# Opening of an expert layer: the residual turned once, the router on the residual, shift and scale applied where gathered rows are turned back

## The reference, cut to what matters

```python
xl = xl + ml[2] * yl                                    # yl = o @ gdn_w_o
hl = _modulate(_rmsnorm(xl, norm_g[1, 1]), ml[3], ml[4])  # h * (1 + scale) + shift
xl = xl + ml[5] * moe(hl)

def moe(h):
    top_v, top_i = lax.top_k(h @ router, 2)
    top_w = softmax(top_v)
    return sum(gate[:, e] * swiglu(h, w_in[e], w_out[e]) for e in range(8))
```

## Time and profile before

| what | value |
|---|---|
| time before, median of 3 | 2807.66 us (2806.9 to 2814.33) |
| the profiled execution, its own time | 2807.92 us |
| its span, first to last instruction | 2805.8 us |
| busy: PE, PEld, DVE, ACT, POOL | 2677.2, 1790.9, 1001.7, 664.5, 523.0 us |
| mean granted TensorE clock | 0.976 |

### The profile page before, as it was taken

How to read it: one execution, slowest core, us unless ns; L and a number is a source line. 1 busy time by engine, 2 the same in 40 slices (tenths; PEclk the granted TensorE clock), 3 DMA queues, 4 the chain that set the end, 5 groups by cost and what they waited for, 6 DMA issues and landing times. The chain is left out here.

```text
span 2805.8 us, 46230 instructions
## 1 busy us (share of the span) xinstructions
PE 2677.2 (95%) x18826; PEld 1790.9 (64%) x18827; DVE 1001.7 (36%) x2298; ACT 664.5 (24%) x1395; POOL 523.0 (19%) x465
## 2 busy tenths in 40 slices
PE   6999999889999999999999999999998999999997
PEld 3555555555555555556677767776557778677784
DVE  2344454227667763113444434443331110000100
ACT  3344444121222210114231333233131010010000
POOL 0111111023233214313233313232100000000000
PEclk8999999899999999999999999999988999999999
DMA  7224222213433332201001110111139995684821
GB/s 241 66 74 124 66 66 77 90 45 90 120 105 110 114 108 70 62 23 32 24 9 32 32 31 2 32 32 31 39 118 368 307 311 185 193 262 156 271 94 31
DMA packets 315616, 297.56 MB, mean 106 GB/s; under 512 B 5824, under 2 KB 277312, under 8 KB 315328
## 3 DMA queue, kind: packets, MB, share of 16 engines
q1 hardware_dynamic: 309408, 273.17, 31.9%
q0 software_dynamic: 4896, 17.83, 2.4%
q10 hardware_dynamic: 1152, 4.19, 0.4%
HBM read 281.01 MB, written 12.58 MB: 105 GB/s over the span
## 5 line engine op out<-in xcount | busy, mean ns | idle before, releaser
L1751 PE MATMUL bank<-work,weight_ring 128*128 128x128 f32 (+1 forms) x2048 | 314.8, 316 | 6.1 <-ACT work L1802 6.1
L2202 PE MATMUL bank<-hidden,weight_ring 128*128 128x512 f32 (+1 forms) x768 | 308.7, 536 | 1.8 <-ACT work L2546 1.8
L1751 PEld LDWEIGHTS bank<-work,weight_ring 128*128 128x128 f32 x2048 | 291.2, 193 | 27.7 <-issue 8.1
L640 PE MATMUL bank<-weight_ring,hidden 128*128 128x384 f32 x760 | 267.6, 497 | 4.8 <-ACT work L768 4.6
L1292 PE MATMUL bank<-hidden,weight_ring 128*128 128x384 f32 x704 | 238.3, 492 | 4.9 <-ACT hidden L425 4.9
L1438 DVE SCALAR_TENSOR_TENSOR weight_ring<-weight_ring,silu_c 128x256 f32<-128x256 f32 x308 | 213.7, 734 | 5.5
L640 PEld LDWEIGHTS bank<-weight_ring,hidden 128*128 128x128 f32 x760 | 138.3, 191 | 109.2 <-ACT work L768 16.6
L1292 PEld LDWEIGHTS bank<-hidden,weight_ring 128*128 128x128 f32 x704 | 133.2, 192 | 93.7 <-issue 7.0
L2202 PEld LDWEIGHTS bank<-hidden,weight_ring 128*128 128x128 f32 x768 | 134.9, 190 | 82.4 <-issue 68.1
L1292 PE MATMUL bank<-weight_ring 128*128 128x384 f32 x528 | 182.3, 496 | 0.3 <-DVE work L1446 0.3
L1908 DVE TENSOR_TENSOR work<-work,bank 128x128 f32<-128x128 f32 (+1 forms) x88 | 29.7, 338 | 424.6 <-ACT work L1807 424.6
(11 more groups left out here) (364 smaller groups left out, 3774.6 us busy)
## 6 DMA issues: line engine op xcount, KB each, us to landing
weight_ring<-in_moe_w_in SPq DMA_DIRECT2D x64, 1024.0 KB, 9.6
weight_ring<-in_ada_w SPq DMA_DIRECT2D x38, 1024.0 KB, 5.3
weight_ring<-in_ffn_w_in SPq DMA_DIRECT2D x44, 512.0 KB, 4.9
hidden<-in_moe_w_out SPq DMA_DIRECT2D x8, 2816.0 KB, 9.9
residual<-in_moe_w_out SPq DMA_DIRECT2D x8, 2816.0 KB, 15.3
work<-in_moe_w_in SPq DMA_DIRECT2D x16, 1024.0 KB, 8.2
weight_ring<-in_na_w_qkv SPq DMA_DIRECT2D x24, 512.0 KB, 7.8
weight_ring<-in_gdn_w_qkv SPq DMA_DIRECT2D x24, 512.0 KB, 5.5
```

The costliest lines, as they stand in the source:

```text
L640: mm = nc.tensor.matmul(m.psum[6][:, 0:3 * P], m.H[:, k, t * P:(t + 1) * P], weights(u)[:, k, :], start=(k == 0), stop=(k == KD - 1))
L1751: mm = nc.tensor.matmul(B[c % 4][:, ab * HALF:ab * HALF + N], w[:, ab, k, (c % 2) * P:(c % 2 + 1) * P], XG[:, k, 0:N], start=(k == 0), sto ...
L2202: mm = nc.tensor.matmul(B[b][:, c0:c0 + t1 - t0], W[:, s, k, :], m.H[:, k, t0:t1], start=(k == 0), stop=(k == KD - 1))
```

## The change

`finish_output` and the last `Norm` go; their work moves into one Block of `experts` in another order.

- The last products and sums (8 each) stand first in `experts`. `X` is turned once, into eight banks (`X_BANKS`), four blocks of features 0 to 3 for each token tile, then 4 to 7; VectorE alone copies the banks into `RT`.
- ScalarE squares the 4 row tiles of 1024 with an accumulated sum, takes the root, VectorE the reciprocal (`ss`, a value for each row).
- `HT` (now in the `hidden` tensor) is `RT` times `ss`: ScalarE tiles 1 and 3, VectorE 0 and 2. Scale and shift are not in it.
- The router runs on the unnormalised `X`, with the scale multiplied into its weights by GpSimd, as four column groups of 32; shift times router is a matmul of its own (`C_ONES`); the logits get `ss` and the shift part on VectorE.
- Scale and shift are applied in `turn`, as 8 ScalarE instructions with a scale and a bias operand in place of 4 copies; TensorE's first chunk waits for them pair by pair.
- SP: slabs 1 to 3 at once, slabs 0 and 4 once the last products are done, slab 5 after the first gather and the store of `out`, then `w_out`.
- ScalarE stores the four tiles of hidden rows after the exponential of the weights, then copies the gains, then stores the four tiles of `out`.

```diff
@@ sync
-            for j in range(SLOTS):
+            for j in range(1, SLOTS):
                 load_slab(0, j)
-            sp.wait_ge(h_stored, 64)
+            sp.wait_ge(last_product, last_0 + KD)
+            load_slab(0, 0)
             load_slab(0, 4)
+            for b in range(2):
+                sp.wait_ge(gathered[b], 16)
             sp.wait_ge(rows_stored, 64)
             load_slab(0, 5)
-            sp.wait_ge(h_turned, 8)
-            sp.wait_ge(logits, 1)
+            sp.wait_ge(h_stored, 64)
             load_out(0, 0)
@@ gpsimd
+            nc.gpsimd.memset(router, 0.0).then_inc(router_ok, 1)
+            nc.gpsimd.tensor_tensor(shift_parts, given, m.MOD[:, 1, 3, :, 0:1].broadcast_to([P, KD, EXPERTS]), ALU.mult).then_inc(shift_ok, 1)
+            pool.wait_ge(router_ok, 1)
+            nc.gpsimd.tensor_tensor(router[:, :, 0:EXPERTS], given, m.MODA[:, 1, 1, :, 0:1].broadcast_to([P, KD, EXPERTS]), ALU.mult).then_inc(router_ok, 1)
             pool.wait_ge(h_stored, 64)
             pool.wait_ge(idx_ok, 1)
             gather()
@@ tensor
-            pre.on_tensor(pe)
...
+            for g in range(KD):
+                if g >= 6:
+                    pe.wait_ge(added, added_0 + g - 5)
+                nc.tensor.matmul(B[g % 6][:, :], m.out_w[g][:, KD - 1, :], m.O[:, KD - 1, :], start=True, stop=True).then_inc(last_product, 1)
+            for n, bank in enumerate(X_BANKS):
+                half, t = divmod(n, 4)
+                pe.wait_ge(added, added_0 + 4 * half + 4)
+                for k in range(4):
+                    mm = nc.tensor.transpose(B[bank][:, k * P:(k + 1) * P], m.X[:, 4 * half + k, CTX + t * P:CTX + (t + 1) * P], ident)
+                mm.then_inc(x_rows, 1)
+            pe.wait_ge(router_ok, 2)
+            pe.wait_ge(rows_out, 2)
+            for kk in range(2):
+                for q in range(4):
+                    mm = nc.tensor.matmul(B[6][32 * q:32 * q + 32, :], router[:, 2 * q + kk, :], m.X[:, 2 * q + kk, CTX:TOK], ...)
             mm.then_inc(logits, 1)
+            pe.wait_ge(shift_ok, 2)
+            nc.tensor.matmul(B[7][:, 32:40], const(m, C_ONES), shift, start=True, stop=True)
             pe.wait_ge(logits_row, 1)
             for t in range(4):
+                mm = nc.tensor.matmul(B[7][:, 8 * t:8 * t + 8], lrow[:, t * P:(t + 1) * P], const(m, C_FOUR, EXPERTS), ...)
@@ tensor, turn
-                pe.wait_ge(x_out, it * 4 + 4)
+                            if (c, ab, k % 2) == (0, 0, 0):
+                                pe.wait_ge(x_out, it * KD + k + 2)
@@ scalar
+            for t in range(4):
+                act.wait_ge(rows_out, 5 + t)
+                nc.scalar.activation(junk, RT[:, t, :], ACT.Square, accum_out=ss[:, t:t + 1]).then_inc(squared, 1)
+                act.wait_ge(squared, squared_0 + t + 1)
+            nc.scalar.activation(ss, ss, ACT.Sqrt, bias=const(m, C_EPS, 1), scale=1.0 / D).then_inc(root, 1)
             act.wait_ge(logits, 1)
+            nc.scalar.copy(lrow, B[6][:, :]).then_inc(logits_row, 1)
+            act.wait_ge(inverted, inverted_0 + 1)
+            for t in (1, 3):
+                nc.scalar.activation(HT[:, t, :], RT[:, t, :], ACT.Identity, scale=ss[:, t:t + 1]).then_inc(rows_scaled, 1)
             act.wait_ge(weights, 1)
             nc.scalar.activation(small[:, 1, :], small[:, 0, :], ACT.Exp).then_inc(route_exp, 1)
+            act.wait_ge(rows_scaled, 4)
...
@@ scalar, turn
-                    nc.scalar.copy(XG[:, 2 * j:2 * j + 2, 0:N], B[j][:, 0:2 * N].rearrange("p (k s) -> p k s", k=2)).then_inc(x_out, 1)
+                    for k in range(2):
+                        nc.scalar.activation(XG[:, 2 * j + k, 0:N], B[j][:, k * N:(k + 1) * N], ACT.Identity, bias=m.MOD[:, 1, 3, 2 * j + k, 0:1],
+                                             scale=m.MODA[:, 1, 1, 2 * j + k, 0:1]).then_inc(x_out, 1)
@@ vector
...
+            dve.wait_ge(shift_ok, 1)
+            nc.vector.tensor_reduce(shift, shift_parts.rearrange("p k e -> p e k"), AX.X, ALU.add).then_inc(shift_ok, 1)
+            dve.wait_ge(root, root_0 + 1)
+            nc.vector.reciprocal(ss, ss).then_inc(inverted, 1)
+            for t in (0, 2):
+                nc.vector.tensor_scalar(HT[:, t, :], RT[:, t, :], ss[:, t:t + 1], None, ALU.mult).then_inc(rows_scaled, 1)
             dve.wait_ge(logits_turned, 1)
...
```

More of the change, by code:

```diff
@@ L111, in constants @@
     c[:, C_SLOT:C_SLOT + 2 * P] = np.arange(2 * P)
-    c[:, C_FOUR:C_FOUR + 2] = row % 32 == np.arange(2)
+    c[:, C_FOUR:C_FOUR + EXPERTS] = row % 32 == np.arange(EXPERTS)
     c[:, C_TOK:C_TOK + 4] = row + P * np.arange(4)
@@ L401, in on_tensor @@
         summed, _, inverted, spread, _, _ = m.norm_sems
[L402 to L407, removed]
+        for t in range(TOK // P):
+            for src in (m.sq_sum, m.sq):
+                mm = nc.tensor.matmul(m.psum[0][:, t:t + 1], src[:, t * P:(t + 1) * P], const(m, C_MEAN, 1), start=(src is m.sq_sum),
+                                      stop=(src is m.sq))
+        mm.then_inc(summed, 1)
         pe.wait_ge(inverted, self.base[2] + 1)
@@ L417, in on_scalar @@
         summed, root, _, _, scaled, hidden = m.norm_sems
-        tiles = slice(self.first // P, TOK // P)
+        tiles = slice(0, TOK // P)
         nc.scalar.activation(self.warm, const(m, C_EPS, 1), ACT.Sqrt).then_inc(root, 1)
@@ L1040, in _ @@
                                             m.psum[1][:, 0:2 * ADA_EARLY].rearrange("p (g v) -> p g v", v=2), b, ALU.add).then_inc(mod_sum, 1)
[L1044 to L1087, removed]
 def swiglu_chunk(m, s):
@@ L1498, in _, with experts @@
                         modulation_scale(m, 1, norm)
-def experts(m, pre):
+def experts(m):
     nc, dram = m.nc, m.dram
@@ L1533, in experts @@
     slab_4, slab_5 = area(IN), area(IN)
-    HT = slab_4.rearrange("p (t d) -> p t d", t=4)
+    last_product, added = m.proj_sems[2:4]
+    _, last_0, added_0 = m.proj_base
+    squared, squared_0 = m.sq_sems[0], m.sq_base[0]
+    _, root, inverted = m.norm_sems[0:3]
+    _, root_0, inverted_0 = m.norm_base[0:3]
+    HT = m.ht[:, 0:4 * D].rearrange("p (t d) -> p t d", t=4)
+    router = m.sc32
+    ss, shift = m.sq_sum[:, 0:4], m.sq_sum[:, 8:8 + EXPERTS]
+    shift_parts = m.sq_sum[:, 16:16 + EXPERTS * KD].rearrange("p (k e) -> p k e", k=KD)
+    given = m.small[:, S_RT:S_RT + EXPERTS * KD].rearrange("p (k e) -> p k e", k=KD)
+    X_BANKS = (6, 7, 2, 3, 4, 5, 0, 1)
     RT = slab_5.rearrange("p (t d) -> p t d", t=4)
@@ L1678, in _ @@
             pe.sem_inc(summed, 2)
-            pre.on_tensor(pe)
[L1681 to L1684, removed]
-            mm.then_inc(logits, 1)
-            for n in range(8):
-                if n >= 4:
-                    pe.wait_ge((h_even, h_odd)[n % 2], (n - 4) // 2 + 1)
-                for k in range(4):
-                    mm = nc.tensor.transpose(B[n % 4][:, k * P:(k + 1) * P],
-                                             m.H[:, 4 * (n % 2) + k, CTX + (n // 2) * P:CTX + (n // 2 + 1) * P], ident)
-                mm.then_inc(h_turned, 1)
+            for g in range(KD):
+                if g >= 6:
+                    pe.wait_ge(added, added_0 + g - 5)
+                nc.tensor.matmul(B[g % 6][:, :], m.out_w[g][:, KD - 1, :], m.O[:, KD - 1, :], start=True, stop=True).then_inc(last_product, 1)
@@ new lines, in _ @@
+            for n, bank in enumerate(X_BANKS):
[8 more added lines that the diff above has]
+                for q in range(4):
+                    mm = nc.tensor.matmul(B[6][32 * q:32 * q + 32, :], router[:, 2 * q + kk, :], m.X[:, 2 * q + kk, CTX:TOK], start=(kk == 0),
+                                          stop=(kk == 1), skip_group_check=True)
@@ L2879, in build @@
         delta_net(m, Norm(m, 1, 0), ahead=delta_net_ahead(m))
-        finish_output(m)
-        experts(m, Norm(m, 1, 1, first=CTX, sums=False))
+        experts(m)
 _INS = ["x", "ctx", "ada_w", "na_w_qkv", "na_w_o", "gdn_w_qkv", "gdn_w_gate", "gdn_w_o", "ffn_w_in", "ffn_w_out",
```

66 lines of the change are left out of this document (28 added, 38 removed).

## The result

| | before | after |
|---|---|---|
| time, median of 4 each | 2807.59 us | 2787.98 us (2785.53 to 2789.38) |
| the profiled execution, its own time | 2807.92 us | 2786.99 us |
| its span | 2805.8 us | 2785.0 us |

The ratio is 0.9924 with a 95% interval of 0.9907 to 0.9941: faster, by 0.6 to 0.9%. The forecast was 2790.8 us with a range of 2785 to 2799. The span fell by 20.8 us where the sum had 17.0.

What follows compares the result with a forecast made beforehand. TensorE was taken to bound the expert turns, with the gain ahead of the first turn. Opening 16.3 plus turns 0.7 gave 17.0 us, from 2807.92 to 2790.9, forecast as 2790.8 us; range 2785 to 2799.

Steps and rivals of the forecast that it cites:

- What bounds the experts, where the gain can lie: Expert turns: TensorE almost throughout, weights no limit; gain lies ahead of the first turn or in gaps at turn starts.
- The opening's steps: Last sum to first turn, priced step by step: first turn starts at 2106.9 in place of 2123.2, 16.3 us earlier.
- What releases the stores: Before the hidden stores: table load ends 2085.5, weights come 2085.4, exponential done 2085.7, first store issued 2085.8.
- Store to gather: After the hidden stores' issue: 12.4 us as before to 2098.2, then 0.9 to the gather's issue.
- The indices: Gain rows to end of pick: 10.6 us, from 2083.7 to 2094.3, leaving the store late by about 4 us.
- The rival that the store hides behind the stream: Hidden store moves behind the weight stream, landing near 2101 to 2106; time 2794 to 2799, say 2796; chance 0.14.
- an instant store gains 4 us: Lower bound for the hidden store: an instant store leaves the indices at 2094.3, 4 us better.
- Slab 0: Weight stream ahead of the first turn: ten half-slabs run until 2093 and, beside the stores, later; slab 0 needed at 2109.
- The turns: Expert turns: 0.5 us lost in each of four narrow, 0.7 won in each of three wide, 0.5 in first; 0.7 won together.
- the rival of one more wide turn: Expert turns: rounding moves a token, an expert goes from 128 to 129 rows, 55.6 us more, 2846 us; chance 0.02.
- TensorE's clock in the turns: Expert turns: forecast stays at 1.00; rival drops to 0.50 at pauses, 2.0 us seven times, 14 us, 2805; chance 0.06.
- The exponential followed the table load at once: Opening: table load 1.28 us with exponential at once; a 1.38 us drain would make the opening's sum -14.9.

Runs made afterwards that it cites:

- e11: Changed kernel with each of the four squares done twice; hidden stores issued at +23.57 us, gather at +35.34 us after the first sum.
- e12: Changed kernel with the router's product done twice; hidden stores issued at +18.03 us, gather at +29.84 us after the first sum.
- e4: Changed kernel with slab 4 asked for only when the hidden rows are stored; hidden stores +18.02 us, gather +29.79 us after the first sum.
- e6: Changed kernel with the four hidden stores put ahead of the exponential; hidden stores +17.39 us, gather +29.71 us after the first sum.
- e8: Changed kernel with slabs asked for only after the eight row copies, order 1, 2, 3, 0, 4; span 2797.0 us.
- e1: Changed kernel with only the finer wait undone: a turn's first chunk waits for all eight scaled pieces; 2808.89 us, a single run.
- e2: Changed kernel with four plain copies per turn, waited for one by one, shift and scale left out; narrow turn 60.92 us, wide 117.28 us.
- e9: Changed kernel with slabs asked for only after the eight row copies, order 0 to 4; span 2785.5 us.
- e10: Changed kernel plus early gain matmuls, hidden stores before the exponential, VectorE scaling the last four feature groups; 2792.16 us, ratio to the kernel before 0.9941.

## Why the prediction was right, point by point

- *What bounds the experts, where the gain can lie*: as read. The first turn starts with the gather's landing, and no later turn waits for weights.
- *The opening's steps* hold nearly one by one up to the stores, counted from the first sum: fifth copy to the first square +9.78 (predicted 9.9), squares done +14.5 (14.7), the row copy of logits done +15.3 (15.6), scaled rows by ScalarE +17.4 (17.9), the router's product in 1.92 us and hidden, hidden stores +18.84 (19.5). e11 shows the squares on the path and e12 the router beside it. No run splits the 17.7 us among the steps that were removed; what is shown is that the new steps take what their rows said.
- *What releases the stores* was taken for the table load, with the weights 0.1 us ahead of it. In the trace the weights (L1814 ends at 2086.07) come 0.14 after the load's end (2084.65 + 1.28) and release exponential and stores together; in e4 and e12, with a faster clock at the logits, the queue issues the first two stores while the load still runs (in e12 2089.31, load from 2088.66 to 2089.94). The load is not in the way of the stores.
- *Store to gather* was sized 13.3 (12.4 and 0.9) and is 11.7 (11.4 and 0.3); *the gather's flight* 7.8 and is 8.6. The 0.9 is the time from the pick's last copy to the gather in the kernel before; behind a landing it is 0.28. The rival that the store hides behind the stream did not come, though ScalarE issued while SP was still issuing (24.71 us for its next four): once started, the store gets 0.65 MB in 2 us and the stream 0.17.
- *The indices* were forecast 4 us ahead of the store; the pick ends at +29.17 in place of +28.0, 1.1 us ahead of the store's landing. Since the gather needs 1.17 us after the pick and 0.28 after the landing, the store was the later by only 0.2 us. The gain and rank matmuls ran at the lower clock, 3.76 and 2.14 us. The bound "an instant store gains 4 us" was too wide: with this pick 0.2 us could be had, and 0.8 in e6, whose pick ended sooner. That the store released the gather, as forecast, hung on those 0.2 us and was luck.
- *Slab 0* was said to be in place by about 2093 for a turn at 2109. It landed at 2100.6 and was used from 2108.2: a margin of 7.6 us in place of 16. The step left out that slab 0 is fourth and that the stores take the engines from it, and e8 shows what that can cost.
- *The turns* were forecast to win 0.7 and won 3.9. Narrow turns lost 0.29 each, not 0.5: the eight instructions take 0.36 us each, not 0.39. Wide ones won 0.97, not 0.7 (0.47 us an instruction in place of 0.49). The timeline of a narrow turn:

```profile
2168.90 1.04 PE L1709 MATMUL bank<-constants,work 128*128 128x128 f32 x8
...
2169.32 2.90 ACT L1773 ACTIVATE work<-bank,modulation,modulation_scale 128x128 f32<-128x128 f32 x8 [16.52 <-PE bank L1709]
...
2170.18 10.06 PE L1723 MATMUL bank<-work,weight_ring 128*128 128x128 f32 x81 [0.24 <-ACT work L1773]
```

  Eight in 2.90 us; TensorE's pairs follow them. The first turn won 2.2, not 0.5; over the runs with the same turns it is 62.65 to 63.98, with the moment at which the clock rises, so 0.9 us is won by the worst of them and up to 1.3 more is that moment; the kernel before has one such trace only. (The 117.4 us that the prediction took for a wide turn runs from a wide turn's first chunk to a narrow one's, which stands earlier in its turn; a whole wide turn is 118.45, so the rival of one more wide turn was worth 56.6 us and not 55.6.)
- *TensorE's clock in the turns* stayed at 1.00, as the forecast had it. e1 shows what the rival needed: pauses of 2.4 us, not 0.2.
- *The exponential followed the table load at once*, here too (0.18 us, and that for the weights), and the load itself began 0.02 us after the last scaled row. The Trainium skill (ScalarE: Activation LUTs, What ACT_TABLE_LOAD costs) adds a drain of 1.38 us; these traces do not show it.

The total was right to 2.8 us. The span's parts are the opening, 1.4 better than its sum, the turns, 3.2 better, and 0.9 lost ahead of the change, which no step could foresee. (The last step of the sum is off by 0.1: 2790.92 less 0.26 is 2790.7, not 2790.8.) That it came so near is in part luck, since one kernel's executions differ by 4 to 10 us.

What stays open: why the first packet of the store comes 4.0 us after its issue, and what the store would take with idle DMA engines, which no run has. Also open is what decides the clock at the turned logits. No run has scale and shift back in the rows together with the new opening and the finer wait; e2 puts the turns' part of it at 5.4 us.

## What to carry to other kernels

Price a moved per-element step by the engine that must do it at the seam: here scale and shift in the norm stood in the chain once, with 0.82 us (L425 before, at 2083.26), and in the turns they cost 1.19 us in each narrow one, where TensorE stood waiting. A wait for the first piece in place of all of them gave 9.5 us over eight turns in one line, and without it this change would have been no gain. When a load is issued in an order forced by a slot that is still in use, look at where the first-needed piece stands in the queue, and at what will share the engines with it: with the same amount in another order, e9 lost nothing of the 10.3 us that e8 waited.

## What the runs showed of the hardware that was not expected

- Behind the same work and the same pause of 3.17 us the eight passes of the turned logits took 1.88 us in some executions and 1.06 in others (e4, e6), and moved the hidden stores by 0.8 us.
- Two DMA queues shared the engines by packets and not by bytes: 175 packets each in 2 us, which was 0.65 MB of hidden rows and 0.18 MB of weights (before, 2102 to 2104).
- Beside a full stream the first packet of a store came 4.0 us after its issue, in the kernel before, the changed one and e4 (2084.21, first packets at about 2088.1).
- In a narrow turn with coarse waits (e1) the clock fell after an idle of 2.4 us in three turns of four, and cost 1.5 to 1.6 us each time.
- ScalarE's queue issues DMAs while a table load ahead of them in the program is still running.
- VectorE's own loop and branch instructions at a turn's start keep it from new work for about 1.3 us after its last small copy (e10).
